# Two transformer blocks on one core: single transposing DMAs behind chunk loads, and block sums split one place earlier, in the first feed-forward

## The reference

```python
    hn = rmsnorm(h, ffn_norm[l])
    h = h + (jax.nn.silu(hn @ w_gate[l]) * (hn @ w_up[l])) @ w_down[l]
```

## Time and profile before

| what | value |
|---|---|
| time, median of 3 runs | 2432.62 us (2431.26 to 2433.0) |
| profiled execution, its own time | 2431.56 us |
| its span, first to last instruction | 2429.8 us |
| mean granted TensorE clock | 0.999 |
| PE busy | 2412.9 us (99%) |
| DVE busy | 1882.3 us (77%) |
| ACT busy | 1418.9 us (58%) |
| DMA from HBM | 456.19 MB, 189 GB/s over the span |

### The profile page before, as it was taken

The page is one execution under the profiler, slowest core; times in us unless marked ns, Lnnn a source line. Parts: engine busy times, 40 slices in busy tenths (PEclk is TensorE's granted clock), DMA queues, the critical chain, the costliest instruction groups (busy, mean ns, idle before and its releaser), DMA issues.

```text
span 2429.8 us, 28901 instructions
## 1 busy us (share of the span) xinstructions
PE 2412.9 (99%) x11057; PEld 1997.5 (82%) x11057; DVE 1882.3 (77%) x2411; ACT 1418.9 (58%) x1766; POOL 50.8 (2%) x93
## 2 busy tenths in 40 slices
PE   9999999999999999999999999999999999999998
PEld 7888888888887878888888888888788888888886
DVE  6455555688888888989777587564789999999877
ACT  6446555445666566666456465564666666666554
POOL 1000110000000000000001100000000000000000
PEclk9999999999999999999999999999999999999999
DMA  7655555656676767677666555566566565656665
GB/s 238 197 172 155 185 156 163 215 192 191 195 213 202 218 203 219 206 209 208 197 208 197 166 156 164 154 192 193 174 194 196 191 199 191 198 192 190 199 216 165
DMA packets 263237, 465.89 MB, mean 192 GB/s; under 512 B 40519, under 2 KB 42737, under 8 KB 262465
## 3 DMA queue, kind: packets, MB, share of 16 engines
q1 hardware_dynamic: 261696, 458.42, 61.1%
q0 software_dynamic: 1376, 5.69, 0.7%
q10 hardware_dynamic: 32, 0.01, 0.0%
HBM read 456.19 MB, written 2.10 MB: 189 GB/s over the span
## 4 chain that ended last, share of the span: by engine, by line
PE 92%; DVE 5%; DMA 2%; ACT 1%; issue 1%; DVEq 0%; SPq 0%; ACTq 0%
PE acc L1033 15%; PE acc L1035 15%; PE acc L1034 15%; PE acc L749 11%; PE acc L751 11%; PE acc L750 11%; PE mis L1033 3%; PE mis L1034 3%; PE mis L1035 3%; DMA wf_raw<-in_w_up 2%; DVE wf L2476 1%; PE mis L1312 1%; PE mis L847 1%; PE mis L722 1%; DVE tf L2483 1%
## 5 line engine op out<-in xcount | busy, mean ns | idle before, releaser
L1623 ACT ACTIVATE wf<-wf_raw 128x1024 fp32r<-128x1024 f32 x544 | 565.0, 1056 | 510.4 <-DVE wf_raw L2464 221.8
L2476 DVE TENSOR_TENSOR wf<-wf_raw,wf 128x1024 fp32r<-128x1024 f32 x544 | 644.6, 1221 | 85.2 <-ACT wf L1623 81.5
L2132 DVE TENSOR_TENSOR lo<-raw,hi 128x1024 fp32r<-128x1024 f32 (+1 forms) x313 | 376.5, 1219 | 231.0 <-ACT hi L1376 228.6
L1376 ACT ACTIVATE hi<-raw 128x1024 fp32r<-128x1024 f32 (+1 forms) x313 | 320.8, 1049 | 165.6 <-PE acc L751 140.0
L1033 PE MATMUL acc<-wf,xb_hi 128*128 128x512 f32 x931 | 364.5, 391 | 0.0
L1035 PE MATMUL acc<-wf,xb_lo 128*128 128x512 f32 x931 | 362.6, 389 | 0.0
L1034 PE MATMUL acc<-wf,xb_hi 128*128 128x512 f32 x931 | 362.2, 389 | 0.0
L749 PE MATMUL acc<-hi,xa_hi 128*128 128x512 f32 (+1 forms) x576 | 224.4, 390 | 0.0
L751 PE MATMUL acc<-hi,xa_lo 128*128 128x512 f32 (+1 forms) x576 | 221.8, 385 | 0.0
L750 PE MATMUL acc<-lo,xa_hi 128*128 128x512 f32 (+1 forms) x576 | 221.6, 385 | 0.0
L749 PE MATMUL acc<-hi,xb_hi 128*128 128x512 f32 x544 | 216.3, 398 | 0.0
(11 more groups left out here) (531 smaller groups left out, 3821.2 us busy)
## 6 DMA issues: line engine op xcount, KB each, us to landing
raw<-in_w_in SPq DMA_DIRECT2D x215, 512.0 KB, 4.0
wf_raw<-in_w_ffn_in SPq DMA_DIRECT2D x160, 512.0 KB, 3.5
wf_raw<-in_w_gate SPq DMA_DIRECT2D x88, 512.0 KB, 3.6
wf_raw<-in_w_up SPq DMA_DIRECT2D x88, 512.0 KB, 4.0
wf_raw<-in_w_down SPq DMA_DIRECT2D x88, 512.0 KB, 3.8
wf_raw<-in_w_ffn_out SPq DMA_DIRECT2D x88, 512.0 KB, 3.7
wf_raw<-in_w_out SPq DMA_DIRECT2D x32, 512.0 KB, 3.9
raw<-in_w_o SPq DMA_DIRECT2D x32, 512.0 KB, 4.8
```

Of the source, the lines that this page charges most:

```text
L1376: nc.scalar.activation(hi[:, slot, :, 0:width], raw[:, slot, :, 0:width], ACT.Copy)\
L1623: nc.scalar.activation(wf[:, f_slot[c], 0, :, :], wf_raw[:, f_slot[c], 1, :, :], ACT.Copy)\
L2132: V.tensor_tensor(lo[:, slot, :, 0:width], raw[:, slot, :, 0:width], hi[:, slot, :, 0:width].bitcast(F32), ALU.subtract).then_inc(lo_ready, 1)
L2476: V.tensor_tensor(wf[:, f_slot[c], 1, :, :], wf_raw[:, f_slot[c], 1, :, :], wf[:, f_slot[c], 0, :, :].bitcast(F32), ALU.subtract).then_inc ...
```

## The change

Three things change, all in the feed-forward of the first block (and in the one boundary of the output projection before it, which shares the helpers).

1. SP: the four transposing DMAs of one pair no longer stand together ahead of chunk(7, 0). The two of plane 0 stand singly behind chunk(7, 0) and chunk(7, 1), the two of plane 1 singly behind chunk(0, 0) and chunk(0, 1) of the pair after. For the last planes the places are k pairs 8 and 9 of `d0`.
2. ACT and DVE: the high and the low part of the block sums of k pair 0 are made ahead of those of chunk(1, 0), where they stood behind them.
3. ACT: `ff_copy` moves behind the high parts of chunk(1, 1) and chunk(2, 0) of the next pair.

```diff
-            def turn_planes(m):
-
-                sp.wait_ge(planes_ok, 2 * m + 2)
+            def turn_plane(m, h, t):
+
+                sp.wait_ge(planes_ok, 2 * m + h + 1)
                 if m:
                     sp.wait_ge(ff_out, m)
-                for h in range(2):
-                    for t in range(TT):
-                        sp.dma_start(tplanes[:, h, :, t * P:(t + 1) * P], planes[:, h, t, :], transpose=True)\
-                            .then_inc(planes_turned, 16)
+                sp.dma_start(tplanes[:, h, :, t * P:(t + 1) * P], planes[:, h, t, :], transpose=True)\
+                    .then_inc(planes_turned, 16)
+
+            def beside_chunk(p, k, h):
+
+                if p in ffn_b and k == 7:
+                    turn_plane(p.i - 1, 0, h)
+                if (p in ffn_b[1:] or p is d0) and k == 0:
+                    turn_plane(FT - 2 if p is d0 else p.i - 2, 1, h)
+                if p is d0 and k in (8, 9):
+                    turn_plane(FT - 1, k - 8, h)
 
             def pair_chunks(p):
 
                 for k in range(p.nk):
-                    if p.stage == "ffn" and p.i and k == 7:
-                        turn_planes(p.i - 1)
-                    if p is d0 and k == 8:
-                        turn_planes(FT - 1)
                     for h in range(2):
...
                             .then_inc(f_in[slot], 16)
+                        beside_chunk(p, k, h)
...
             def first_chunks(p):
                 f_hi_of(p, 0, 0)
                 f_hi_of(p, 0, 1)
-                f_hi_of(p, 1, 0)
                 if 0 in p.forms:
                     t_hi_of(p, 0)
+                f_hi_of(p, 1, 0)
...
                 first_chunks(after)
-                ff_copy(p.i - 1)
                 f_hi_of(after, 1, 1)
                 f_hi_of(after, 2, 0)
+                ff_copy(p.i - 1)
...
                 f_lo_of(after, 0, 0)
                 f_lo_of(after, 0, 1)
+                t_lo_of(after, 0)
                 f_lo_of(after, 1, 0)
-                t_lo_of(after, 0)
                 finish(p)
                 finish_up(p)
```

## The result

The changed kernel takes 2435.82 us (median of 20 runs), the kernel before 2432.03 (20 runs): a ratio of 1.0017, 95% interval [1.001, 1.0023]. I had forecast 2428.4 and a range up to 2433.2. The forecast was wrong in its sign.

A forecast was written before the change was run, and what follows sets the result against it. PE was taken as the bound, busy 2412.9 of 2429.8 us, so only boundary waits could shrink: 0.46 x 9 = 4.2 us off 2431.56 gives 2427.4, plus 1.06 to the median: 2428.4, range 2423.5 to 2433.2.

The forecast's parts named there:

- The pool: PE's idle time at nine pair boundaries of the first feed-forward: 9.0 us in all, 1.0 each, the most to gain.
- What chunk(7, 1) costs: Load at the pair's end: would land in 3.4 to 3.9 us, against 3.8 needed, so its wait was taken as gone.
- What is late next: Chunk(0, 1) of the next pair, needed by the first block sum, must land 10.9 us ahead of `c12`.
- The landing of chunk(0, 1): SP's queue: issued at about 716.25, landing at 720.9, 4.65 us later, leaving `c12` 0.43 late instead of 0.91.
- break-even: Chunk(0, 1) landing 5.13 us after its issue, the point where `c12` is as late as before the change.
- The sum: Nine boundaries losing 0.54 us instead of 1.0 each: 4.2 us gained, profiled execution 2427.4, median 2428.4.
- this side: Slower rival: chunk(0, 1) takes more than 5.13 us; at 5.8, 6 us worse in all, 2439; chance 0.07.
- The order on ACT and DVE: `tf`'s parts made ahead of chunk(1, 0)'s: `c12` would wait what `q5` no longer waits; costed at zero.
- The copy into `ff_raw`: On ACT, now behind chunk(2, 0)'s high part: gate 1.5 us later but covered by 0.2; costed at zero.
- The transposing rule: Skill's claim that transposing DMAs are as fast as regular ones: about 0.1 us each by estimate, against 0.47 in the rows.
- all gone: Rival: chunk(0, 1) lands within 4.2 us of issue, no boundary wait left, gain 8 to 9 us, 2424; chance 0.22.

The follow-up runs named there:

- fastest kernel: Changed kernel with all four transposing DMAs behind the chunks of k pairs 1 and 2, `ff_raw` copy behind chunk(2, 1), old order of `tf`'s parts: 2422.40 us, 0.996 to before.
- Plane 1 at k 1: Changed kernel with plane 1's two transposing DMAs behind chunk(1, 0) and chunk(1, 1) instead of chunk(0, 0) and chunk(0, 1): 2428.19 us, 0.9986 to before.
- one left: Changed kernel with only the first transposing DMA kept behind chunk(7, 0), the others behind chunk(1, 0), chunk(1, 1), chunk(2, 0): 2423.95 us, 0.9968 to before.
- splits only: Kernel before with only the edits on ACT and DVE, the four transposing DMAs still together: 2432.88 us, 1.0002 to before.

## Why the prediction was wrong

- **The pool.** 9.0 us at nine boundaries: right. The fastest kernel got it back, to 0.3 or 0.4.
- **What chunk(7, 1) costs.** I took this term as gone, with 3.4 to 3.9 to its landing. It lands 4.0 after its issue in the mean (3.4 to 3.6 in the kernels with nothing around it). By itself that would put `c12` at 3.6, 0.2 late, so the term was halfway right; it was no longer the last. "Plane 1 at k 1", where chunk(7, 1) is the later one at most boundaries, has `c12` at 3.75.
- **What is late next.** Right: chunk(0, 1), issued 3.8 behind chunk(7, 1) in the mean (3.7 forecast), and 10.95 from its landing to `c12` (10.9 forecast).
- **The landing of chunk(0, 1): the step that failed.** I wrote that it comes 4.65 after the issue; it took 5.46. My sum was 7.3 for three loads, 0.95 for two transposing DMAs ahead and 0.1 for one behind, 8.35 behind the issue of chunk(7, 1). It was 9.24. Without DMAs between them the loads of this stage take 7.5 to 7.7, not 7.3, which I had from a single boundary of the other feed-forward (the nineteen bursts of three loads 1.36 apart in that stage take 7.5 in the mean); and the three DMAs add 1.5 to 1.7 instead of 1.05. I charged the one behind 0.1, for which no row spoke, where the two ahead had 0.47 each. Three at 0.47 would have made 1.4 and, with 7.6 for the loads, 9.0, which is past the break-even. What is left of the 9.24 is about the scatter of such means. One by one the prices are less even: the one behind chunk(7, 1) adds 0.5 (8.1 in "plane 1 at k 1" against 7.5 in "one left"), the two of plane 1 another 1.2, and no run has only the one behind chunk(0, 1).
- **The sum.** With the landing measured, my own formula gives the result: -6.2 + 10.9 is 4.7, against 4.27 before, 0.47 at each of nine boundaries, 4.2 us. The break-even that I had put at 5.13 after the issue was about right (4.98 from the means). Even the landing of chunk(0, 1) before, 5.1 in the mean and 5.3 and 5.8 in the earlier trace rows, stood at or above it, and I still gave this side 0.07. I should have asked why a chunk would land sooner with more between it and its neighbours than it did before.
- **The order on ACT and DVE** at zero: right, by "splits only" and by the fastest kernel. **The copy into `ff_raw`** at zero: right; the nine boundaries hold the whole difference of the spans.
- **The transposing rule** of the Trainium skill ("Advanced Engine Details and Errata", "X-Bar Transpose (TRN2)"), that transposing DMAs are as fast as regular ones, did not speak against a wait: my estimate from it was wrong. I gave one a sixteenth of a load's bytes; it moves 128 KB, a quarter. By the rate of the fastest kernel's loads above, that is 0.47 us for each instead of 0.1, an estimate, and the 0.47 of the earlier trace rows agrees with the rule instead of overruling it. So one of the two grounds for the rival "all gone" was a wrong number. Between loads the three plain copies add 0.9 to 1.1 us in all and the three transposing ones 1.5 to 1.7; how much of the 0.6 between them is the 1.0 by which the transposing ones hold up SP isn't separated, so these runs don't show that transposing is slower in the queues.
- **The order of the landings** in the earlier trace rows tests nothing: the four count up one semaphore, and the profile gives its counts to the issues in their order.

## What to carry to other kernels

Ask of every small DMA first how many bytes it moves, from the shape in the code (here a quarter of a load), and then which loads stand around it: in a gap of 2.7 us it cost no time, four in a row behind the last load of a burst cost 1.5 to 2.5 us over the whole kernel, and a single one for each boundary inside the burst about 3 to 4. Look at the share of the DMA engines in that very stretch as well; at 0.9, as here, what is slipped in makes the next landing later. And where two chains end at the same wait, price the second at its own worst measured value before counting the gain on the first.

## What I had not expected of the hardware

- A plain copy of 128 KB from SBUF to SBUF between loads delays them by 0.3 to 0.4 us (0.9 to 1.1 for three), somewhat less than the 0.47 that its bytes would take at the loads' rate. It holds SP 0.60 us in 512 pieces and 0.47 in 128; a transposing DMA of the same bytes holds it 1.19 in most rows and up to 1.30 in the earlier trace rows.
- A load that goes out at once behind a transposing DMA (at 715.30 and 717.22 in the changed kernel) holds SP 0.58 to 0.60 instead of 0.37. One that first waits a microsecond for its slot, as at 713.58, holds it 0.38.
- A DMA can delay the load that stands ahead of it in the queue. Chunk(7, 1) takes 3.8 with one transposing DMA ahead and none behind ("one left"), and 4.0 to 4.1 with the same ahead and one behind (four kernels). In the profiled execution of the changed kernel chunk(1, 1) to chunk(2, 1) also took 4.1 to 4.2 to land (3.4 to 3.5 before), though the last transposing DMA had landed before chunk(1, 1) was issued at six of the nine boundaries, and before chunk(2, 0) at all nine. Why is open; no wait hung on them.
